# Products of 64x64 tiles of a gated recurrence put together every second side tick

## The reference

```python
def step(state, blk):                       # chunks of 64 tokens, 8 heads of 64 keys and 64 values
    q_b, k_b, lf_b, v_b = blk
    cum = jnp.cumsum(lf_b, axis=2)
    diff = cum[:, :, :, None, :] - cum[:, :, None, :, :]
    decay = jnp.exp(jnp.where(causal, diff, -jnp.inf))
    scores = jnp.einsum('bhid,bhjd,bhijd->bhij', q_b, k_b, decay)
    o = (jnp.einsum('bhij,bhjv->bhiv', scores, v_b)
         + jnp.einsum('bhid,bhdv->bhiv', q_b * jnp.exp(cum), state))
    last = cum[:, :, -1:, :]
    state = (jnp.exp(last[:, :, 0, :])[..., None] * state
             + jnp.einsum('bhjd,bhjv->bhdv', k_b * jnp.exp(last - cum), v_b))
    return state, o
```

## Time and profile before

| | |
|---|---|
| median of three runs | 2149.15 us |
| profiled execution | 2149.4 us, its span 2147.7 us |
| PE busy | 2126.3 us, 99% of the span |
| DVE busy | 1227.2 us, 57% |
| ACT busy | 914.9 us, 43% |
| POOL busy | 138.4 us, 6% |
| chain that ended last | PE 93%, DVE 3%, ACT 2% |

### The profile page before, as it was taken

How to read it: one execution, slowest core, us unless ns; L and a number is a source line. 1 busy time by engine, 2 the same in 40 slices (tenths; PEclk the granted TensorE clock), 3 DMA queues, 4 the chain that set the end, 5 groups by cost and what they waited for, 6 DMA issues and landing times.

```text
span 2147.7 us, 27329 instructions
## 1 busy us (share of the span) xinstructions
PE 2126.3 (99%) x10932; PEld 1685.7 (78%) x10932; DVE 1227.2 (57%) x1807; ACT 914.9 (43%) x1449; POOL 138.4 (6%) x174
## 2 busy tenths in 40 slices
PE   9999999999999999999999999999999999999999
PEld 7768777678888888887777888888877667888887
DVE  5684774565544444565577555555556676555554
ACT  4464444554433322434455433333445655333332
POOL 0000422111000000010011000000011100000000
PEclk9999999999999999999999999999999999999999
DMA  4213212123232232222112222223221112222223
GB/s 170 87 52 89 61 53 94 40 81 116 98 98 90 97 100 96 99 95 73 60 50 79 89 99 98 98 98 98 88 89 60 59 40 98 98 99 98 89 98 108
DMA packets 52109, 186.91 MB, mean 87 GB/s; under 512 B 5904, under 2 KB 6160, under 8 KB 51856
## 3 DMA queue, kind: packets, MB, share of 16 engines
q1 hardware_dynamic: 51840, 184.99, 25.9%
q10 hardware_dynamic: 144, 0.18, 0.0%
HBM read 183.05 MB, written 2.10 MB: 86 GB/s over the span
## 4 chain that ended last, share of the span: by engine, by line
PE 93%; DVE 3%; ACT 2%; issue 1%; DMA 0%; SPq 0%; DVEq 0%; ACTq 0%
PE ps L1033 24%; PE ps L1036 23%; PE ps L1039 23%; PE ps L1057 4%; PE ps L1060 4%; PE ps L1058 4%; PE ps L1012 3%; PE ps L1110 1%; PE ps L1162 1%; PE ps L1365 1%; PE ps L1383 1%; PE ps L1134 1%; PE ps L1180 1%; PE ps L1255 1%; PE ps L1313 0%
## 5 line engine op out<-in xcount | busy, mean ns | idle before, releaser
L1442 ACT CAST wh<-raw 128x1024 fp32r<-128x1024 f32 x334 | 350.9, 1051 | 864.0 <-PE ps L1039 787.5
L1795 DVE TENSOR_TENSOR wl<-raw,wh 128x1024 fp32r<-128x1024 f32 (+2 forms) x338 | 414.4, 1226 | 173.3 <-ACT wh L1442 172.6
L1033 PE MATMUL ps<-hh,wh 128*128 128x512 f32 x1408 | 448.6, 400 | 1.9 <-DVE F L1933 0.7
L1036 PE MATMUL ps<-hh,wl 128*128 128x512 f32 x1408 | 435.1, 390 | 2.3 <-DVE wl L1795 2.3
L1039 PE MATMUL ps<-hl,wh 128*128 128x512 f32 x1408 | 434.5, 390 | 0.0
L1036 PEld LDWEIGHTS ps<-hh,wl 128*128 128x128 f32 x1408 | 264.2, 188 | 59.1 <-DVE wl L1795 3.6
L1033 PEld LDWEIGHTS ps<-hh,wh 128*128 128x128 f32 x1408 | 257.7, 188 | 67.1 <-issue 15.8
L1039 PEld LDWEIGHTS ps<-hl,wh 128*128 128x128 f32 x1408 | 264.5, 188 | 56.1 <-DVE hl L1876 0.2
L1033 PE MATMUL ps<-R,wh 128*128 128x512 f32 x896 | 286.4, 400 | 0.0
L1036 PE MATMUL ps<-R,wl 128*128 128x512 f32 x896 | 277.5, 390 | 0.5 <-DVE wl L1795 0.5
L1039 PE MATMUL ps<-R,wh 128*128 128x512 f32 x896 | 277.1, 390 | 0.0
(11 more groups left out here) (226 smaller groups left out, 1995.2 us busy)
## 6 DMA issues: line engine op xcount, KB each, us to landing
raw<-in_weights SPq DMA_DIRECT2D x332, 512.0 KB, 3.2
x<-in_x_t SPq DMA_DIRECT2D x4, 512.0 KB, 7.4
F<-in_x_t SPq DMA_DIRECT2D x4, 512.0 KB, 4.3
out<-x SPq DMA_DIRECT2D x8, 256.0 KB, 2.0
raw<-in_weights SPq DMA_DIRECT2D x4, 416.0 KB, 3.2
x<-in_bias SPq DMA_DIRECT2D x1, 1024.0 KB, 7.7
F<-in_weights SPq DMA_DIRECT2D x2, 384.0 KB, 3.6
F<-in_weights SPq DMA_DIRECT2D x2, 256.0 KB, 4.0
```

What stands on the lines that cost most here:

```text
L1033: pe.matmul(out, hi[:, k, cs], B.tile(u.src, k)[0], start=k == 0, stop=False)
L1036: pe.matmul(out, lo[:, k, cs], B.tile(u.src, k)[0], start=False, stop=False)
L1442: act.copy(B.wh[s][:, 0:nk * ncol], B.raw[s][:, 0:nk * ncol]).then_inc(S["w_hi"], 1)
L1795: dve.tensor_tensor(lo, src, hi.bitcast(F32), ALU.subtract).then_inc(S[name], 1)
```

## The change

The schedule of `hgrn` is written anew. Products are issued in every second side tick: levels 0 and 1, then level 2 and the state, then 3 and 4, then 5, 6 and the carry; the value products of a pair stand ahead of levels 0 and 1 of the next. DVE's masked copies and the state chain become steps of their own (`h_take`, `h_carried`) and stand in the side tick behind. Weighings, parts, exponentials and the steps that end a pair move with them. There are 33 side ticks for four pairs, the sum for pair 0 stands one tick earlier, and the ratio is 45 side ticks to 48 dense ones. The functions on DVE keep their bodies; PE's program does not change at all.

```diff
--- before.py
+++ after.py
@@ -412,41 +412,32 @@
         for p in range(4):
             yield [("h_turn", p)]
         for tt in range(4):
-            yield [("h_decay", tt)] + {2: [("h_sum", 0)], 3: [("h_part", 0, 1)]}.get(tt, [])
-        exps = [(p, lv) for p in range(4) for lv in (1, 2, 3, 7, 4, 5, 6)]
-        ends = []
-        yield [("h_zero",), ("h_part", 0, 2), ("h_exp", *exps.pop(0))]
-        yield [("h_weigh", 0, 1), ("h_part", 0, 3), ("h_exp", *exps.pop(0))]
-        weigh = [(0, 2)]
-        for p in range(4):
-            for lv in range(8):
-                tick = [("h_weigh", *w) for w in weigh]
-                weigh = []
-                part = {1: (p, 4), 2: (p, 5), 3: (p, 6), 4: (p + 1, 1), 5: (p + 1, 2), 7: (p + 1, 3)}.get(lv)
-                if part is not None and part[0] < 4:
-                    tick.append(("h_part", *part))
-                if lv == 3 and p < 3:
-                    tick.append(("h_sum", p + 1))
-                if ends:
-                    tick.append(ends.pop(0))
-                if lv < 7:
-                    tick.append(("h_score", p, lv))
-                    if lv == 2:
-                        tick.append(("h_state", p))
-                    if lv == 4:
-                        tick.append(("h_query", p))
-                    if lv == 6:
-                        tick.append(("h_carry", p))
-                else:
-                    tick.append(("h_out", p))
-                    ends += [(n, p) for n in ("h_sq", "h_ms", "h_fin", "h_low")]
-                if exps and lv < 7:
-                    tick.append(("h_exp", *exps.pop(0)))
-                    if tick[-1][2] < 7:
-                        weigh = [tick[-1][1:]]
-                yield tick
-        for e in ends:
-            yield [e]
+            yield [("h_decay", tt)] + {1: [("h_sum", 0)], 3: [("h_part", 0, 1)]}.get(tt, [])
+        yield [("h_zero",), ("h_part", 0, 2), ("h_exp", 0, 1)]
+        yield [("h_weigh", 0, 1)]
+        for t in range(33):
+            p, i = t // 8, t % 8
+            part = {0: (p, 3), 1: (p, 4), 2: (p, 5), 3: (p, 6), 5: (p + 1, 1), 7: (p + 1, 2)}.get(i)
+            weigh = {1: (p, 2), 2: (p, 3), 3: (p, 4), 4: (p, 5), 5: (p, 6), 7: (p + 1, 1)}.get(i)
+            exps = {0: (2,), 1: (3, 7), 2: (4,), 3: (5,), 4: (6,), 6: (1,)}.get(i, ())
+            products = {0: (("h_score", 0), ("h_score", 1)), 2: (("h_score", 2), ("h_state",)),
+                        4: (("h_score", 3), ("h_score", 4)), 6: (("h_score", 5), ("h_score", 6), ("h_carry",))}.get(i, ())
+            takes = {1: (0, 1), 3: (2,), 5: (3, 4), 7: (5, 6)}.get(i, ())
+            ends = {0: ("h_out", "h_sq"), 1: ("h_ms",), 2: ("h_fin",), 4: ("h_low",)}.get(i, ())
+            tick = [("h_weigh", *weigh)] if weigh and weigh[0] < 4 else []
+            tick += [("h_part", *part)] if part and part[0] < 4 else []
+            tick += [("h_sum", p + 1)] if i == 3 and p < 3 else []
+            tick += [(n, p - 1) for n in ends if p]
+            if p < 4:
+                tick += [("h_take", p, lv) for lv in takes]
+                tick += [("h_carried", p)] if i == 3 else []
+                tick += [("h_query", p)] if i == 5 else []
+                tick += [(n, p, *lv) for n, *lv in products]
+            q = p + (i == 6)
+            tick += [("h_exp", q, lv) for lv in exps if q < 4]
+            yield tick
+        for n in ("h_ms", "h_fin", "h_low"):
+            yield [(n, 3)]
 
     def mla(self):
 
@@ -580,9 +571,9 @@
         self.run(made[36:])
         self.banks = (0, 1)
         recurrence = list(self.hgrn())
-        self.run(interleave(self.dense(uGA), iter(recurrence[:-4]), 44 / 48, False))
+        self.run(interleave(self.dense(uGA), iter(recurrence[:-3]), 45 / 48, False))
         self.banks = (0, 1, 4, 5)
-        self.run(self.dense(uC, {2 + 2 * i: t for i, t in enumerate(recurrence[-4:])}))
+        self.run(self.dense(uC, {2 + 2 * i: t for i, t in enumerate(recurrence[-3:])}))
         self.banks = (2, 3)
         self.run(interleave(self.dense(uGB), self.mla(), 83 / 48))
         self.banks = (0, 1, 2, 3)
@@ -2152,7 +2143,7 @@
         dve.tensor_tensor(B.h_queries(n).rearrange("p (b j) -> p b j", j=64 >> lv), later_half(B.f4("F4")[:, p, :], lv),
                           later_half(B.h_decays(n), lv), ALU.mult).then_inc(S["hg_q"], 1)
 
-    def h_state(p):
+    def h_carried(p):
         state, _ = B.k_state()
         two, e = [B.bank[b] for b in h_pair(p, 7)], B.V(2)
         at.wait_ge("hg_u", p + 1)
@@ -2172,7 +2163,7 @@
         at.wait_ge("hg_st", 7 * (p + 1))
         dve.tensor_tensor(e, e, B.f4("F4")[:, p, :], ALU.mult).then_inc(S["hg_tq"], 1)
 
-    def h_score(p, lv):
+    def h_take(p, lv):
         _, Sc = B.k_state()
         at.wait_ge("con2", 16)
         at.wait_ge("hg_z", 1)
...
```

More of the change, by code:

```diff
@@ L2275, in vector_program @@
     todo = {"late": late, "late2": late2, "split_low": split_low, "open": open_part, "first": first, "add": add, "root": root, "root2": root2, "xfin": xfin, "column": column,
-            "merge": merge, "ev": ev, "ev_low": ev_low, "ev2": ev2, "bf": bf, "at": attn, "df": diff, "df_soft": diff_soft, "h_turn": h_turn, "h_decay": h_decay, "h_part": h_part, "h_weigh": h_weigh, "h_state": h_state, "h_query": h_query,
-            "h_score": h_score, "h_fin": h_fin, "h_low": h_low, "c_norm": c_norm, "c_turn": c_turn, "c_qt": c_qt, "c_kv": c_kv,
+            "merge": merge, "ev": ev, "ev_low": ev_low, "ev2": ev2, "bf": bf, "at": attn, "df": diff, "df_soft": diff_soft, "h_turn": h_turn, "h_decay": h_decay, "h_part": h_part, "h_weigh": h_weigh, "h_carried": h_carried, "h_query": h_query,
+            "h_take": h_take, "h_fin": h_fin, "h_low": h_low, "c_norm": c_norm, "c_turn": c_turn, "c_qt": c_qt, "c_kv": c_kv,
             "c_kt": c_kt, "sb": sb, "dn_sum": dn_sum, "dn_mul": dn_mul}
```

## The result

The changed kernel takes 2155.07 us (median of 10 runs, 2153.88 to 2155.38), the kernel before 2149.18 (median of 10, 2149.00 to 2149.33). The ratio is 1.0026, with a 95% interval of 1.0018 to 1.0035: slower by 5.9 us where 1.0 us less was forecast, and outside the range of 2143.5 to 2151.8. The profiled run is the quickest of the ten, 2153.88 us.

What follows compares the result with a forecast made beforehand. PE, busy 2126.3 of 2147.7 us, was taken as the bound. Switching saved 5.2 us and old waits 3.7, new waits cost 7.9: 1.0 less, 2148.1 us after the median's 0.25 offset, range 2143.5 to 2151.8.

Steps and rivals of the forecast that it cites:

- Less switching on PE: Recurrence stretch: 17 visits to 64x64 tiles instead of 32, at 0.35 us each, saving 5.2 us (4.8 to 5.5).
- The old waits: PE's three waits for query weighings in the recurrence stretch, 3.7 us in all, taken as gone.
- New waits: PE waiting behind DVE's ordered steps in the recurrence stretch: 7.9 us taken, bounds 5.7 and 10.5.
- the nine places: Spots in the recurrence of pairs 0 to 3 where PE was forecast to wait, 5.75 us without slowing of DVE.
- the walk: Step-by-step addition of DVE's and PE's times at each place in the recurrence, giving 5.75 us of waits without slowing.
- the three long chains: DVE's step sequences in pairs 1 to 3, 10 to 15 us long, each able to grow by 0 to 1.4 us.
- the first group: First score group of the recurrence: could wait up to 0.5 us for its first weighing, now a tick earlier.
- the slow rival: Same as Rival 2: DVE and POOL meet at every step in pairs 1 to 3, 2154.0 us, chance 0.08.
- Rival 2: Chains of pairs 1 to 3: DVE and POOL meet at every step, 8.0 us more waits, 2154.0 us; chance 0.08.
- Rival 1: Recurrence stretch: waits stay short because DVE has slack and catches up, 3.9 us of waits, 2144.2 us; chance 0.20.
- Rival 3: PE's joined groups: joining saves nothing and only the waits change, 4.2 us slower, 2153.3 us; chance 0.03.

Runs made afterwards that it cites:

- e4: Changed kernel with POOL nearly idle in pairs 1 to 3, one block of eight weighed and a constant for its decay parts; 2147.93 us.
- e9: The changed kernel timed again, unchanged, for the spread of its runs and a second profile; 2154.48 us.
- e3: Kernel before, with only levels 0, 3 and 5 multiplied and copied one tick later, joined with 1, 4 and 6; 2150.83 us.
- e5: e1 with scaling, gating, the result's low half and the next pair's sum moved to later ticks; 2146.75 us.
- e8: e5 with weighing 6 moved to the end of tick 4, ahead of the next weights' low half; 2146.79 us.
- e7: e1 and e4 together on the changed kernel: copies in their products' tick and POOL nearly idle; 2143.53 us.
- e1: Changed kernel with masked copies and state chain back in the side tick of their products; 2146.82 us.
- e6: Changed kernel with only the copies of levels 5 and 6 back in the tick of their products; 2152.58 us.
- e2: Changed kernel with the copy of level 2 and the state chain put first in their tick; 2152.25 us.

## Why the prediction was wrong

**Less switching on PE: right.** 15 visits fewer at 0.35 us. The joined levels 3 and 4, one visit saved, measured 1.66 - 1.25 = 0.41.

**The old waits: right.** None of the three is left.

**New waits: this step failed, in three ways.** Eight of the nine places were named, and the booked waits were 10.5 us against 7.9 taken, at the upper bound of 10.5 that the text gave. The longest, 1.90 at level 3 of pair 3, was not: by the walk's own steps the copy of level 2 is over at about 7.3 and PE wants its bank at 7.8. The wait of level 5 in that pair (0 to 0.5) did not come. With the booked waits alone the sum would be 8.9 - 10.5, 1.6 us slower, 2150.7 and inside the range; what carried the time out of it are two terms that the text put at nothing, the unbooked waits (1.6) and the clock (2.7).

First, copies. A masked copy was taken at 0.34 us for every level. Those of levels 5 and 6 took 1.47 together in the changed kernel. The trace of before already had them at 0.72 and 0.73. DVE's timeline in pair 0, before and then after:

```profile
240.50 0.72 DVE L2191 COPY_PREDICATED F<-C,ps 128x256 f32<-128x256 uint32 x1
...
243.06 0.73 DVE L2191 COPY_PREDICATED F<-C,ps 128x256 f32<-128x256 uint32 x1
```

```profile
245.21 1.47 DVE L2182 COPY_PREDICATED F<-C,ps 128x256 f32<-128x256 uint32 x2
```

The value products waited 1.64 us instead of 0.9.

Second, the slowing by POOL. The prediction allowed each of the three long chains 0 to 1.4 us of growth and took about half (2.15 for the three and the first group). Measured against e4, where POOL is nearly idle, they grew by 1.35, 1.9 and 1.5: pair 1 waited 2.3 us against 0.94, pair 2 2.35 against 0.46, pair 3 3.3 against 1.8. That is at the upper bound of 1.4 or over it. DVE's timeline in pair 3, from weighing 3 to the start of the state chain:

```profile
299.15 0.43 DVE L2143 TENSOR_TENSOR F<-F 128x256 f32<-128x256 f32 x1 [0.85 <-ACT F L1651]
299.50 0.95 DVE L2134 TENSOR_TENSOR F<-C 128x256 f32<-128x256 f32 x1
300.37 0.74 DVE L2186 SCALAR_TENSOR_TENSOR F<-ps,G,F 128x512 f32<-128x512 f32 x1
301.15 1.23 DVE L2192 TENSOR_TENSOR F<-F 128x512 f32<-128x512 f32 x1
302.30 0.83 DVE L2143 TENSOR_TENSOR F<-F 128x256 f32<-128x256 f32 x1
303.05 1.08 DVE L2134 TENSOR_TENSOR F<-C 128x256 f32<-128x256 f32 x1
...
304.39 0.21 DVE L2155 COPY F<-ps 128x64 f32<-128x64 f32 x1
```

Two parts at 0.95 and 1.08, a weighing at 0.83, and the gating at 1.23 us. The same steps with POOL nearly idle, in e4:

```profile
296.65 0.43 DVE L2143 TENSOR_TENSOR F<-F 128x256 f32<-128x256 f32 x1 [1.33 <-ACT F L1651]
...
298.16 0.69 DVE L2192 TENSOR_TENSOR F<-F 128x512 f32<-128x512 f32 x1
...
299.17 0.41 DVE L2134 TENSOR_TENSOR F<-C 128x256 f32<-128x256 f32 x1
...
299.83 0.21 DVE L2155 COPY F<-ps 128x64 f32<-128x64 f32 x1
```

In pair 3 of the changed kernel POOL starts at 299.25 on the exponential on which DVE started at 299.15, and then works to 303.86 with pauses of under 0.2 us, so every step of DVE up to the part at 303.05 has one of POOL's beside it. In a chain that starts from an exponential that both wait for, a meeting is no matter of chance. The rule of the Trainium skill (SBUF — State Buffer, on two separate sides), which the prediction named for the slow rival, points the right way: VectorE with two inputs from SBUF and GpSimd exclude each other for an instruction's length. The scaling, one of whose two tensors comes from PSUM, stayed at 0.74.

Third, waits that are not booked as idle were no term: 1.6 us.

One reading of the walk was wrong without a price: in pair 1 it has the sum get the scaling's bank at 7.4, but by its own steps the scaling is over at 6.5, and without POOL the sum waited only 0.32 (e4). What it lost there it would have found at level 4.

**The clock: missing altogether.** No step of the prediction and no rival had it. It is 1.5 us in the profiled run, the quickest of its ten; the median run is 1.2 longer still (2155.07 - 2153.88) at a lower mean clock, which makes 2.7. The second part is inferred from that mean alone. In e9's series the median was 0.6 lower, with the same waits. The granted clock fell right behind PE's longest waits, 1.90 and 1.36 close together here, 1.78 in e3, 1.80 in e5.

**The sum.** With what was measured: 5.2 saved and 3.7 freed, less 10.5 and 1.6 of waits and 2.7 of clock, is 5.9 slower; the medians say 5.9. The close match is partly luck: the 4.7 of the stretch arrived as 4.4 in the span, and the profiled run of before is 0.2 over its median.

**Rivals.** Rival 2 gave 2154.0 and had the mechanism that decides, DVE and POOL meeting on the chains of pairs 1 to 3, at a chance of 0.08. That its number came near is luck: its price of 8.0 was too high (4.8 by e4), and the unbooked waits and the clock, which it lacked, made up for it. Against it the text said that many steps in the trace of before met nothing; that was read from the whole stretch, while the chains that PE waits for were the ones that met. Rival 1 needed waits under 4 us; the changed kernel had 10.5, and only e5 (3.6), e8 (3.9) and e7 (2.4), with the copies back, came there. Rival 3 falls by the starts of the joined groups.

## What to carry to other kernels

When a change makes PE wait closer behind a queue that is 80% busy, add up that queue between its last forced stop and the wait with the durations that its steps have beside their neighbour, not with their best ones, and take each form's own row. A step moved behind an eviction costs what the eviction waits for, not only what it takes. And a wait of PE such as the 1.8 us of e3 and e5, or two close together, can have a second price, the lower clock behind it, of 1.5 to 1.6 us. The kernel that beats both here is the changed one with its copies and the state chain back in their own tick (e1, 2146.8 us, or e5 at 2146.75). The joins alone, in the old order, did not beat the kernel before (e3).

## What the runs showed of the hardware

A granted clock of 0.57 to 0.80 of full speed in a window of 4 us appeared behind idle times of PE of 1.8 to 3.3 us (the changed kernel twice, e3, e5, e6, e8), and it came or stayed away in different runs of one program: 1.6 us a time in e3 and e5, with nothing else in the order changed. Waits of 1.77 in the profiles of e1 and e2 were not followed by it. The eight runs of e7, whose longest wait is 1.0 us, agree within 0.2; those of the kernels with a wait of about 1.8 or more, or two close together, spread over 1.5 to 3.3. The line between is not sharp: the kernel before, longest wait 1.50, took 2150.7 to 2150.9 us at a mean clock of 0.999 in 3 of the 33 runs beside e1 to e4, and e4, longest wait 1.64, has 1.000 in all of its 11.
